# The second unit's choice of experts made ahead of the second context chunk's residual add and norm

## The reference, cut to what matters

```python
q = (t @ w_query).reshape(nt, 8, 2, 128)
s1, s2 = scores of both halves against 128 keys each
v1, i1 = top_k(s1, 16);  v2, i2 = top_k(s2, 16)
cand = v1[:, None] + v2[None, :]            # 16 x 16 sums per token and head
top_s, top_pos = top_k(cand, 16)
expert_idx = (i1 * 128 + i2)[top_pos];  gates = softmax(top_s)
out = sum over 8 heads x 16 experts of gate * gelu(t . u[expert]) * v[expert]
```

## Time and profile before

| | us |
|---|---|
| median of three runs | 2382.85 |
| range of the runs | 2382.24 to 2383.22 |
| span of the profiled execution, first to last instruction | 2381.6 |
| around that span, up to the median (the profiled execution's own total is not listed) | 1.25 |
| TensorE busy | 1635.9 (69%) |
| VectorE busy | 1553.1 (65%) |
| ScalarE busy | 850.6 (36%) |
| GpSimd busy | 922.6 (39%) |

### The profile page before, as it was taken

The page is one execution under the profiler, slowest core; times in us unless marked ns, Lnnn a source line. Parts: engine busy times, 40 slices in busy tenths (PEclk is TensorE's granted clock), DMA queues, the critical chain, the costliest instruction groups (busy, mean ns, idle before and its releaser), DMA issues.

```text
span 2381.6 us, 27280 instructions
## 1 busy us (share of the span) xinstructions
PE 1635.9 (69%) x9141; PEld 719.9 (30%) x9141; DVE 1553.1 (65%) x3642; ACT 850.6 (36%) x2538; POOL 922.6 (39%) x832
## 2 busy tenths in 40 slices
PE   7998887777867576768564655578787755545664
PEld 3654543323333222323211211125454311111111
DVE  1226667887756667867867665544867877766554
ACT  2223444345443232434323523233433332332322
POOL 1112344534443444444544444410243544444441
PEclk8999998989888888888768878779998877787677
DMA  9997899999999999999999999982599999999996
GB/s 383 391 363 290 358 401 412 417 418 415 415 417 357 420 418 420 418 419 419 422 421 417 421 421 421 421 348 89 229 397 417 419 420 421 422 421 421 421 421 253
DMA packets 165116, 928.41 MB, mean 390 GB/s; under 512 B 17376, under 2 KB 51968, under 8 KB 59888
## 3 DMA queue, kind: packets, MB, share of 16 engines
q0 software_dynamic: 112816, 807.16, 82.2%
q1 hardware_dynamic: 52016, 119.50, 13.3%
q10 hardware_dynamic: 144, 0.01, 0.0%
HBM read 925.46 MB, written 1.15 MB: 389 GB/s over the span
## 4 chain that ended last, share of the span: by engine, by line
DMA 48%; PE 26%; DVE 14%; issue 5%; ACT 4%; POOL 3%; SPq 0%; POOLq 0%; DVEq 0%; ACTq 0%
DMA arena<-in_uv,small 45%; PE bank L1277 11%; DVE arena L2135 6%; PE bank L723 3%; POOL arena L662 3%; PE bank L688 2%; ACT aux L1530 2%; PE bank L143 1%; DMA arena<-in_w_o 1%; PE bank L709 1%; PE bank L870 1%; DMA arena<-in_ada 1%; PE bank L1103 1%; DVE aux L2057 1%; PE bank L700 1%
## 5 line engine op out<-in xcount | busy, mean ns | idle before, releaser
L1277 PE MATMUL bank<-arena,aux 64*64 64x512 f32 x6016 | 955.0, 783 | 649.4 <-ACT aux L1530 612.3
L662 POOL DMA_INDIRECT arena<-in_uv,small x764 | 887.5, 1162 | 1256.9 <-PE bank L1277 919.6
L2135 DVE CUSTOM_DVE_ANT_0 arena<-arena,h 128x1024 f32<-128x1024 f32 x764 | 921.4, 1225 | 502.6 <-DMA arena<-in_uv,small 496.7
L1277 PEld LDWEIGHTS bank<-arena,aux 64*64 64x64 f32 x6016 | 271.8, 175 | 1278.8 <-ACT aux L1530 728.9
L1523 ACT ACTIVATE small<-small 128x4 f32<-128x4 f32 (+2 forms) x198 | 40.6, 205 | 1172.7 <-DVE small L2135 1172.5
L1514 ACT ACTIVATE aux<-small 128x64 f32<-128x64 f32 x768 | 204.4, 337 | 11.3 <-DVEq L2126 2.6
L1530 ACT ACTIVATE aux<-aux,small 128x64 f32<-128x64 f32 x768 | 204.9, 336 | 6.8 <-ACT small L1523 0.5
L723 PE MATMUL bank<-hT,aux 128*128 128x256 f32 (+1 forms) x752 | 165.0, 377 | 5.0 <-DMA aux<-in_w_query 2.7
L723 PEld LDWEIGHTS bank<-hT,aux 128*128 128x128 f32 x752 | 135.3, 199 | 48.5 <-issue 27.7
L1486 ACT ACT_TABLE_LOAD x67 | 86.0, 1283 | 1.2
L2135 DVE DVE_READ_ACCUMULATOR2_ANT small<- 128x1 f32 x768 | 62.5, 81 | 0.0
(11 more groups left out here) (262 smaller groups left out, 1559.9 us busy)
## 6 DMA issues: line engine op xcount, KB each, us to landing
arena<-in_ada SPq DMA_DIRECT2D x36, 1024.0 KB, 10.6
aux<-in_w_query SPq DMA_DIRECT2D x43, 512.0 KB, 8.1
arena<-in_uv,small POOLq DMA_INDIRECT x764, 17.6
hT<-in_ada SPq DMA_DIRECT2D x7, 1024.0 KB, 9.6
arena<-in_w_o SPq DMA_DIRECT2D x7, 1024.0 KB, 13.7
arena<-in_w_uq SPq DMA_DIRECT2D x16, 384.0 KB, 13.0
arena<-in_w_qkv SPq DMA_DIRECT2D x3, 2048.0 KB, 9.5
h<-in_ada SPq DMA_DIRECT2D x5, 1024.0 KB, 11.1
```

Of the source, the lines that this page charges most:

```text
L662: nc.gpsimd.indirect_dma_start(out=slot_at(pos), out_offset=None, in_=d["uv"][unit // FIRST], in_offset=bass.IndirectOffsetOnAxis(ap=self. ...
L1277: last = nc.tensor.matmul(bank[2 * r + m][out:out + 64, :], self.dg[rr, (s + o) % 8, :], slot_at(at)[rr, cols], start=first, stop=False)
L2135: last = nc.vector.tensor_tensor_reduce(out=slot_at(at)[:, 0:D], in0=slot_at(at)[:, 0:D], in1=h[:, c * D:(c + 1) * D], scale=1.0, scalar=0 ...
```

## The change

Both maxima of unit 1 and all three stages of its choice move from the loop (stage 1 stood at group 0, stages 2 and 3 at group 1 of unit 0) to a place right behind the dots of unit 0 group 0, ahead of `ada_rows(5)`, `add_mix(1)` and the norm of chunk 1. The number of instructions stays as it was, and no other engine's program is touched. The removed branches served unit 0 alone, since unit 32, the other unit with `start_of`, leaves the loop before it.

```diff
                 finish_gates(0)
                 dots(0, 0, range(GRP))
+                dve.wait_ge(sc_done, 2)
+                for side in range(2):
+                    tops(1, side, S_BANK[:, (2 * side + 1) * NKEY:(2 * side + 2) * NKEY])
+                dve.sem_inc(tops_done, 1)
+                for stage in (1, 2, 3):
+                    choose(1, stage)
                 ada_rows(LAYERS * ADA_ROUNDS - 1)
                 add_mix(1, (bank[6], bank[7]), self.mix_rows[:, 0], y_done, (6, 6))
                 ffn_rstd(1)
                 norm_rows(1, self.mix_rows[:, 1], self.gate_f, hf_ready)
...
                         if start_of(n):
-                            if g == 0:
-                                dve.wait_ge(sc_done, 2)
-                                for side in range(2):
-                                    tops(n + 1, side, S_BANK[:, (2 * side + 1) * NKEY:(2 * side + 2) * NKEY])
-                                dve.sem_inc(tops_done, 1)
-                                choose(n + 1, 1)
-                            if g == 1:
-                                choose(n + 1, 2)
-                                choose(n + 1, 3)
                             if g == 3:
                                 finish_gates(n + 1)
```

## The result

The change made the kernel slower: 2394.64 us median of four runs (2392.26 to 2396.29) against 2382.55 us (2381.68 to 2383.22) before, a ratio of 1.0051 with a 95% interval of 1.0039 to 1.0063. That is half a percent, 12.1 us; the forecast was 2393.1, 10.2 us of shift. The profiled execution took 2395.19 us around a span of 2393.1.

A forecast was written before the change was run, and what follows sets the result against it. DMA bytes were taken to set the pace for most of the span, but TensorE's chain in this stretch; +10.24 us, other terms 0, on the 2381.6 span gave 2391.8, plus 1.25 around it 2393.1 us, range 2387.5 to 2397.

The forecast's parts named there:

- The block is 10.24 us: Work moved on VectorE for unit 1: maxima 3.81 us, stage 1 3.60, stages 2 and 3 2.83, together 10.24.
- The path runs through the norm of chunk 1: Before gather 12: residual add, norm, transposes, queries, scores, combine, place free, gather; VectorE's work on unit 1 lies beside it.
- four consequences: Behind the late `ada_rows(5)`: late `combine(0, 0)`; row store and gathers 10.2 us later; late add and norm; later TensorE work.
- The third and fourth: Residual add and norm of chunk 1 late, transposes 216.75 to about 227.0; then `combine(0, 1)` to 242.6, gather 12 to 245.4.
- the change lies in such a hole: Claimed the change sits where DMA is not full: share 0.77 from 178 to 237 us, 0.51 from 227 to 237.
- The relief on VectorE buys 0: Group 1's dots, freed of the stages, end about 239, ahead of the score copy at 240.2: 0 gained, at most 10.24.
- Earlier indices buy 0: Unit 1's indices, ready near 217.5 instead of 231, gain 0; gather 16 used them only at 249.15.
- TensorE's clock: First query of chunk 1, 5.47 us at half clock: change taken as 0, bounds 1.6 us back or 1.6 added.
- Nothing is caught up later: Behind 245 us the same programs run 10.2 us late; holes of at most 11.5 us, recovery taken as 0.
- Rival A: Delay absorbed in DMA holes from 237 to 297 us: up to 11.5 us back, 2381.6 to 2383; chance 0.11.
- rival B: Group 1's combine waited for VectorE's dots: up to 6.4 us back there; chance 0.02 of faster by over 0.2%.
- Rival C: Longer idle time costs two slow spells (+1.6 us each), or loads and gathers meet less well: 2394.7 to 2397; chance 0.12.

The follow-up runs named there:

- Run 1: The whole block behind the last modulation rows and ahead of the residual add of chunk 1, against the kernel before: 2393.93 us, ratio 1.0046.
- Run 3: Kernel before with only the maxima of unit 1 (3.81 us) moved ahead of the modulation rows, the three stages left in place: 2385.51 us, ratio 1.0019.
- run 5: Kernel before with the residual add of chunk 1 made between the second and third dot of unit 0 group 0: 2379.80 us, ratio 0.9990.
- run 2: The whole block right behind the norm of chunk 1, ahead of the dots of group 1, against the kernel before: 2383.91 us, ratio 1.0005.
- run 4: Kernel before with stage 1 of unit 1's choice done twice in its old place, 3.6 us more VectorE work: 2382.89 us, ratio 1.0005.
- run 6: Kernel before with throwaway TensorE products, 14 behind the last modulation products and 12 behind `combine(0, 0)`: 2380.83 us, ratio 0.9989.
- run 8: Kernel before with the early residual add and throwaway TensorE products (14 behind the modulation products, 4 behind `combine(0, 0)`): 2377.70 us, ratio 0.9975.

## Why the prediction was right, point by point

1. **The block is 10.24 us.** Measured 10.3 (207.16 to 217.46). Right.
2. **No idle time of VectorE is filled, and the scores are there.** The maxima followed the last dot without a gap (207.16). Right.
3. **The path runs through the norm of chunk 1.** Run 1 shows it: with the store, the combine and gathers 7 to 10 back in time, the loss stayed (1.0046). Run 3 gives the dose (3.8 us for 3.81) and run 5 the other sign. The prediction listed four consequences without saying which of them carries the loss. The third and fourth do; the first, the late `combine(0, 0)`, was 2.07 us short of doing so too. One thing was loose: "the change lies in such a hole". The DMA share was 0.90 from 207 to 217 us; the hole came at 231.
4. **The relief on VectorE buys 0.** Right in the changed kernel: the Gelu of group 1 waited for nothing of VectorE's. The margin was far wider there than forecast. The prediction had the dots of group 1 done by about 239, from its bound of 14.6 us on gather 7; that gather, sent at 222.75, was there for its dot at 230.05, and the dots ended at 231.3, 9.9 us ahead of the score copy. In the old place the cover is thin: 2.8 us beside the slow query, 1.2 beside a fast one. In runs 2 and 4, where more work stood ahead of the dots, the Gelu waited 1.62 and 2.39 us for them.
5. **Earlier indices buy 0.** Right, gather 16 went out 43 us after they were ready.
6. **TensorE's clock, taken as 0 between -1.6 and +1.6.** This is the term that was mis-sized, inside its bounds. The reason given for 0, that the idle time right before the query is unchanged, does not hold: after 2.92 us (before) and 2.07 us (changed) of idle time ahead of the transposes the query was slow, after 1.86 and 2.46 us (runs 2 and 4) it was fast. The bounds were too narrow as well, since 5.47 us is a query slow in part; in run 1 it took 6.51. In the profiled execution the term was +0.87 on the query (6.34 less 5.47), and the transposes took 1.46 instead of 1.09; with the 10.2 of the block, and dots that ended 0.2 us earlier, this makes the 11.2 us at gather 12. Later low spells moved the shift between 11 and 14 us.
7. **Nothing is caught up later.** Right by the medians (12.1 us, and 11.7 in run 1). The 11.2 us at gather 12 and 11.16 at gather 767 agree better than two executions can be trusted to. The 1.25 us that the sum adds around the span is a median less the span of another execution; in the changed kernel's own it was 2.1.
8. **Rival A, absorbed in the holes up to 297 us.** Shown wrong: the holes moved along with the work, since what they wait for is TensorE's order. The prediction cited the Trainium skill, "Perfetto Trace Analysis", section "Identifying Performance Opportunities", by which improving a kernel generally means improving its most-contended engine; the same section adds that this engine can change from one regime of a kernel to the next. The runs agree with it only in that form, stretch by stretch: DMA is that engine over the span, but 10 us of VectorE, 65% busy, cost 12 us here, and 2.9 us moved the other way (run 5) were worth 2.4 (0.2 to 4.5). Of rival B, VectorE as the path, the changed kernel shows nothing: its group 1 was ready and waited.
9. **Rival C, the clock adds.** It was given 0.12 and the measured 2394.64 lies just short of its lower edge, at the upper edge of the forecast's own range; the excess over 10.2 is 1.9 us, against a spread of 4 us among the four runs. How much of that excess is the clock stays open by the times alone.

## What to carry to other kernels

Moving work ahead of something costs its whole length if that something is on the path, whatever the average busy shares say; ask first who waits for the instruction that is pushed back, not who waits for the one that is pulled forward. Where two suspects slide together (here a queue and a norm), put the moved block between them: the run tells whether the second alone is enough. It does not tell that the first alone would be free; that takes the reverse order. A DMA that is full later did not forgive a delay made before it fills, and it passed on a saving too (2.9 us at gather 12 and 2.8 at the last one in run 5).

## What had not been expected of the hardware

TensorE's low clock spells are not a property of the program alone. The same first query took 5.47 us in the kernel before and 3.84 in runs 2 and 4, with the whole program ahead of it unchanged up to the norm; `combine(0, 0)` took 5.36, 6.34 and 5.75 us. The Trainium skill, "TensorE: Matmul & The Clock Gate", section "Part 1: The HAM clock gate (the "warmup" mystery)", says that how many matmuls run slow at the start of one and the same kernel differs from run to run; the rows show the same for spells in the middle of one. With throwaway products in the gaps `combine(0, 0)` was fast in runs 6 and 8 (3.66 us in both), but the query still met a spell in run 6 (5.32 us), and it was fast in run 5 without any. So the products did not settle where the spells fall. A forecast of one execution so has a term of a us or two for each query or combine on the path that only its bounds can hold.
